# MLP weight groups with seven products: buffers of their own, other places, and 24 instead of 32 of them

## The chip, the cores and the metric

The kernel runs on one core of a Trainium2 chip. The metric is the device time of one execution in microseconds (us). The median of three runs of the kernel before is 1685.07 us (1681.4 to 1685.62). One more execution was recorded by the hardware profiler.

## What is computed

One decoder layer on 256 tokens of width 2048, all in float32. The change touches its last part only, the MLP:

```python
h2 = _rms(x, norm2_g)
x = x + jnp.square(jax.nn.relu(h2 @ w_up)) @ w_down
```

`w_up` is 2048 x 8192 and `w_down` 8192 x 2048. Before it, three token mixers (a gated convolution, forgetting attention, cross-attention to 256 memory tokens) are projected from x, gated, merged and multiplied by `w_out`.

## The kernel before

**Precision.** Each float32 operand is split in two parts of the type float32r: the upper part is a copy (ScalarE, `whi`), the lower part the difference between the value and the upper part (VectorE, `wlo`). A product takes three matmuls: lower x upper, upper x upper, upper x lower.

**Pieces and rings.** Weights stream from HBM in pieces of 256 rows x 512 columns (128 partitions x 2 x 512, 512 KB). There are four raw buffers, four of `whi` and four of `wlo` (RING = 4), all used by piece number modulo 4. SyncE issues the load of piece n when the lower part of piece n - 4 is made (L404 to L407, semaphore `lo_ready`). ScalarE makes the upper part of piece n (`split`, L527) when it has landed and TensorE has used piece n - 4 (`piece_used`); VectorE then makes the lower part (L882). Each engine works its queue strictly in the order in which it is written down.

**The MLP** is cut in 4 quarters of 4 blocks. Blocks 0 and 1 of a quarter multiply by `w_up` (1024 columns each), blocks 2 and 3 by `w_down`, with the quarter's activations as the left operand. A block has 8 groups (GROUPS) of 256 rows, each with a left and a right piece. A plain group (`half_group`, L1601) is 24 matmuls of 128x512. Groups 3 and 6 (`FAST`) are computed in another way (`fast_group`, L1621): a 2x2 by 2x2 block product with seven products instead of eight, 21 matmuls. It needs sums of weight blocks (`t_sums`, L1187 to L1192, VectorE, from the raw ring), their upper parts (`sums_hi`, L730, ScalarE) and lower parts (`sums_lo`, L1196, VectorE), the upper and lower parts of three of the four weight blocks (`split_fast`, L740 and L1203), and sums of the left operand (`s_sums`, `s_hi`, `s_lo`).

**Banks.** Of the eight PSUM banks, 0 to 3 hold the block's four results (C22, C12, C21, C11), 4 to 7 the products P5, P6, P7 and P1, which are summed over the block's two fast groups and combined with the rest at its end: ScalarE copies P1 (L835) and banks 0 to 3 (`c_copy`, L803), VectorE combines (`combine`, L1208 to L1212) and adds (`result`, L1230; for blocks 2 and 3 `x_to_sums`, L1224, first). Behind an up block, relu and square are taken (ScalarE, L813 and L816), and while the next block runs TensorE transposes the activations into banks 4 to 7 (`act_transposes`, L1406), from where ScalarE (`act_hi`, L707) and VectorE (`act_lo`, L920) take them. So the first fast group of a block must wait until the combination of the block before and these takings are done.

**Order.** VectorE's queue in a block (some lines left out), which fixes what stands behind a wait:

```python
                    left(blk, 2)
                    t_sums(ff_piece(q, blk, 3), 2 * at, base=by_8, base16=by16)
                    right(blk, 2)
                    sums_lo(2 * at, base=by_8)
                    if after_up:
                        act_lo(blk, 0)
                    fast(blk, 3)
                    if after_up:
                        act_lo(blk, 1)
                    left(blk, 4)
```

`left` and `right` make the lower part of a group's pieces, `fast` that of a fast group.

Of the kernel before, what the change touches and what calls it, by code (L numbers as in the profile page):

```python
# [18 lines left out]
F32 = mybir.dt.float32  # L19
# [137 lines left out]
FAST = (3, 6)  # L157
# [7 lines left out]
T_3, T_1, T_2, T_4 = range(4)  # L165


def ff_piece(q, blk=0, g=0):

    return first(B_FF) + FF_PIECES * q + 2 * (GROUPS * blk + g)  # L170
# [47 lines left out]
def build(nc, t, out):  # L218
    ctx = ExitStack()
    with ctx:  # L220
# [22 lines left out]
        with ExitStack() as mlp_only:  # L243
            comb = mlp_only.enter_context(nc.sbuf_tensor("comb", [P, 5, COLS], F32))
        y_parts, conv = two_views("y_parts", [P, 2, CW // P, TOK * P], F32R,
                                  "conv", [P, 2, CW // P, TOK * P], F32)
        with ExitStack() as mlp_only:
            def mlp(name, shape, dt):
                return mlp_only.enter_context(nc.sbuf_tensor(name, shape, dt))
            t_raw = mlp("t_raw", [P, 4, COLS], F32)  # L250
            t_hi = mlp("t_hi", [P, 4, COLS], F32R)
            t_lo = mlp("t_lo", [P, 4, COLS], F32R)
            s_up = mlp("s_up", [P, 2, len(FAST), 4, P], F32R)
            s_down = mlp("s_down", [P, 2, len(FAST), 4, P], F32R)
            s_raw = mlp("s_raw", [P, len(FAST), 4, P], F32)
            a_raw = mlp("a_raw", [P, len(FAST), 4, P], F32)
# [94 lines left out]
        t_used = sem("t_used")  # L351
# [13 lines left out]
        w_down = t["w_down"].rearrange("(q k p) n -> q p k n", p=P, k=KT)  # L365

# [32 lines left out]
        def _(sp):  # L399
# [66 lines left out]
            for n in range(ff_piece(0), ff_piece(1)):  # L466
                blk, g, side = (n - ff_piece(0)) // (2 * GROUPS), (n // 2) % GROUPS, n % 2
                k = slice(PK * g, PK * (g + 1))
                if blk < UPS:
                    load(n, w_up[:, k, WIDE * blk + COLS * side:WIDE * blk + COLS * (side + 1)])  # L470
                else:
                    at = WIDE * (blk - UPS) + COLS * side
                    load(n, w_down[0, :, k, at:at + COLS])

            with sp.Fori(0, QUARTERS - 1) as i:
                for n in range(ff_piece(1), ff_piece(2)):
                    blk, g, side = (n - ff_piece(1)) // (2 * GROUPS), (n // 2) % GROUPS, n % 2
                    k = slice(PK * g, PK * (g + 1))
                    if blk < UPS:
                        src = w_up[:, k, bass.ds(i * D + (D + WIDE * blk + COLS * side), COLS)]  # L480
                    else:
                        at = WIDE * (blk - UPS) + COLS * side
                        src = w_down[bass.ds(i + 1, 1), :, k, at:at + COLS].rearrange("q p k n -> (q p) k n")
                    load(n, src, base=i * FF_PIECES)
# [35 lines left out]
        def _(act):  # L520
            def split(n, base=0, base16=0):


                act.wait_ge(landed[n % RING], base16 + 16 * (n // RING + 1))
                if n >= RING:
                    act.wait_ge(piece_used, base + (n - RING + 1))
                act.activation(whi[n % RING], raw[n % RING], ACT.Copy).then_inc(hi_ready, 1)  # L527
# [183 lines left out]
            def a_copy(bk, u, gain=None):  # L711

                for j in range(PK):
                    last = act.activation(a_raw[:, u, 2 * j:2 * j + 2, :],
# [5 lines left out]
            def s_hi(i, u, dst, base=0):  # L720
                act.wait_ge(s_made, base * 4 + 4 * (i + 1))
                act.activation(dst[:, 0, u], s_raw[:, u], ACT.Copy).then_inc(s_hi_ready, 1)

            def sums_hi(i, base=0):

                if i is not None:
                    act.wait_ge(t_used, base + i)
                for h in range(2):
                    act.wait_ge(t_made, base * 3 + (3 * (i or 0) + 1 + 2 * h))
# [3 lines left out]
            def split_fast(n, base=0, base16=0):  # L733

                for u in range(2):
                    act.wait_ge(landed[(n + u) % RING], base16 + 16 * ((n + u) // RING + 1))
                act.wait_ge(piece_used, base + (n + 2 - RING))
                r = n % RING
                src, dst = [w[:, r:r + 2, :].rearrange("p r n -> p (r n)")[:, COLS:] for w in (raw_all, whi_all)]
                act.activation(dst, src, ACT.Copy).then_inc(hi_ready, 2)  # L740

            def wo_events(n):

                for j in range(NBD):
# [10 lines left out]
                    for a in range(2):  # L755
                        if n == e + 6 + a:
                            g, pair = G_X2 + 2 * j + a, 2 * j + a
                            if pair in FAST:
                                act.wait_ge(tr_made, g + 1)
                                a_copy(tr_bank(g), FAST.index(pair), R_N2 + PK * pair)  # L760
                            operand_hi(g, lhs_b, PK * pair, R_N2)
                if n == end(B_WO + FAST[0] // 2) + 10:
# [14 lines left out]
            def quarter(q, i):  # L777

                by_n, by16, by_b, by_8 = i * FF_PIECES, i * (FF_PIECES * 16 // RING), i * FF_BLOCKS, i * (2 * FF_BLOCKS)

                def left(blk, g):
                    split(ff_piece(q, blk, g), base=by_n, base16=by16)
                    if q == 0:
                        wo_events(ff_piece(q, blk, g))

                def right(blk, g):
                    split(ff_piece(q, blk, g) + 1, base=by_n, base16=by16)
                    if q == 0:
                        wo_events(ff_piece(q, blk, g) + 1)

                def fast(blk, g):
                    split_fast(ff_piece(q, blk, g), base=by_n, base16=by16)
                    if q == 0:
                        for side in range(2):
                            wo_events(ff_piece(q, blk, g) + side)

                def c_copy(blk, side):

                    at = FF_BLOCKS * q + blk
                    act.wait_ge(piece_used, by_n + (ff_piece(q, blk) - 1 + side))  # L800
                    act.wait_ge(ff_done, by_8 + 2 * (at - 1))
                    act.wait_ge(tr_made, by_8 + (G_FF + GROUPS * (q if blk else q - 1) + 4 * min((blk - 1) % FF_BLOCKS, UPS)))
# [15 lines left out]
                def act_hi(blk, side):  # L818
                    for a in range(2):
                        pair = 4 * (blk - 1) + 2 * side + a  # L820
                        g = G_FF + GROUPS * q + pair
                        if pair in FAST:
                            act.wait_ge(tr_made, by_8 + (g + 1))
                            a_copy(4 + 2 * side + a, FAST.index(pair))
                        plain_hi(g, PK * pair, act_parts, bk=4 + 2 * side + a, base=by_8)

                for blk in range(FF_BLOCKS):
                    after = q > 0 or blk > 0
                    after_up = 0 < blk <= UPS
                    at = FF_BLOCKS * q + blk  # L830
                    left(blk, 0)
                    if after:
                        act.wait_ge(piece_used, by_n + (ff_piece(q, blk) - 2))
                        act.wait_ge(ff_done, by_8 + 2 * (at - 1))
                        act.activation(comb[:, 3, :], bank[P1], ACT.Copy).then_inc(p1_copied, 1)  # L835
                    right(blk, 0)
                    if after:
                        c_copy(blk, 0)
                        c_copy(blk, 1)
                    left(blk, 1)  # L840
                    right(blk, 1)
                    if after_up:
                        relu_square(blk, 0)
                    left(blk, 2)
                    if after_up:
                        relu_square(blk, 1)
                    right(blk, 2)
                    sums_hi(2 * at, base=by_8)
                    if after_up:
                        act_hi(blk, 0)  # L850
# [867 lines left out]
```

## Time and profile before

| | us |
|---|---|
| median of 3 runs | 1685.07 |
| lowest, highest | 1681.4, 1685.62 |
| profiled execution | 1689.01 |
| its span, first to last instruction | 1687.3 |
| PE (matmuls) busy | 1642.3 |
| VectorE busy | 1104.8 |
| ScalarE busy | 851.2 |

The numbers behind an engine are the time in which it works, and PE's matmuls overlap: one lasts 390 ns and the next begins 227 ns after it. A wait is idle time ahead of an instruction, with what ended it. The granted clock is the share of TensorE's full clock (2.4 GHz) that the chip allowed; its other level is 1.2 GHz. "L882" is line 882 of the kernel before.

### The profile page before, as it was taken

How to read it: one execution, taken by the hardware profiler on the slowest of the kernel's cores; microseconds unless marked ns; L12 is line 12 of the kernel's file. 1: busy time of each engine (PE TensorE's matmuls, PEld its weight loads, DVE VectorE, ACT ScalarE, POOL GpSimd, SP SyncE). 2: the span in 40 equal slices, each digit the busy share in tenths (PEclk: the TensorE clock that was granted, in tenths of full speed). 3: DMA queues.
4: the chain of work that ended last, by engine and by line, in shares of the span. 5: the costliest groups of instructions: out<-in, count | busy, mean ns of one | idle time of the engine just before them, and what ended most of it. 6: DMA issues, size and time to landing. Idle time of an engine off the chain costs nothing.

```text
span 1687.3 us, 20278 instructions
## 1 busy us (share of the span) xinstructions
PE 1642.3 (97%) x7404; PEld 1354.5 (80%) x7404; DVE 1104.8 (65%) x1199; ACT 851.2 (50%) x1002; POOL 4.8 (0%) x13
## 2 busy tenths in 40 slices
PE   9999999999999999999999999999999999999997
PEld 7888888888888888888888877778777777877876
DVE  5856666555564444466656777777777786778777
ACT  6744444444454444444445566545554465446643
POOL 0000000000000000000000000000000000000000
PEclk9999999999999999999999999999999999999999
DMA  9856555565666666665566555466555555555554
GB/s 332 276 169 188 171 154 172 162 171 167 175 180 191 192 189 196 197 190 188 182 192 187 173 188 184 154 193 194 171 177 175 181 182 182 189 182 182 182 181 149
DMA packets 160190, 313.70 MB, mean 186 GB/s; under 512 B 9584, under 2 KB 9968, under 8 KB 159600
## 3 DMA queue, kind: packets, MB, share of 16 engines
q1 hardware_dynamic: 160112, 312.62, 60.2%
q8 instruction: 54, 0.88, 0.2%
q14 instruction: 24, 0.20, 0.0%
HBM read 310.49 MB, written 2.10 MB: 185 GB/s over the span
## 4 chain that ended last, share of the span: by engine, by line
PE 79%; DVE 8%; DMA 7%; issue 4%; ACT 1%; SPq 0%; DVEq 0%; ACTq 0%
PE bank L1389 51%; PE bank L1601 17%; PE bank L1621 8%; DMA raw<-in_w_down 4%; DVE wlo L882 3%; DMA raw<-in_w_up 2%; PE bank L1406 1%; DVE t_raw L1187 1%; ACT whi L527 1%; PE bank L1419 1%; DVE comb L1224 1%; DVE t_raw L1190 1%; DMA raw<-in_w_mem_kv 1%; DVE lhs_a L920 0%; DVE wlo L1203 0%
## 5 line engine op out<-in xcount | busy, mean ns | idle before, releaser
L882 DVE TENSOR_TENSOR wlo<-raw,whi 128x1024 fp32r<-128x1024 f32 x510 | 622.0, 1224 | 486.5 <-ACT whi L527 483.4
L527 ACT ACTIVATE whi<-raw 128x1024 fp32r<-128x1024 f32 x510 | 535.6, 1059 | 577.5 <-PE bank L1389 393.6
L1389 PE MATMUL bank<-whi,lhs_a 128*128 128x512 f32 x1920 | 598.2, 393 | 0.0
L1389 PEld LDWEIGHTS bank<-whi,lhs_a 128*128 128x128 f32 x1920 | 357.3, 188 | 71.7
L1389 PE MATMUL bank<-wlo,lhs_a 128*128 128x512 f32 x960 | 374.8, 390 | 0.0
L1601 PE MATMUL bank<-whi,lhs_a 128*128 128x512 f32 x768 | 238.5, 392 | 9.8 <-DVE wlo L882 9.8
L1601 PE MATMUL bank<-whi,lhs_b 128*128 128x512 f32 x768 | 238.5, 392 | 4.9 <-DVE wlo L882 4.9
L1389 PEld LDWEIGHTS bank<-wlo,lhs_a 128*128 128x128 f32 x960 | 180.3, 188 | 38.0
L1601 PEld LDWEIGHTS bank<-whi,lhs_a 128*128 128x128 f32 x768 | 143.1, 188 | 42.1 <-DVE wlo L882 13.2
L1601 PEld LDWEIGHTS bank<-whi,lhs_b 128*128 128x128 f32 x768 | 143.1, 188 | 36.3 <-DVE wlo L882 7.4
L1389 PE MATMUL bank<-whi,lhs_b 128*128 128x512 f32 x512 | 158.3, 391 | 2.7 <-DVE wlo L882 1.7
L1601 PE MATMUL bank<-wlo,lhs_b 128*128 128x512 f32 x384 | 149.8, 390 | 0.0
L1601 PE MATMUL bank<-wlo,lhs_a 128*128 128x512 f32 x384 | 149.8, 390 | 0.0
L730 ACT ACTIVATE t_hi<-t_raw 128x1024 fp32r<-128x1024 f32 x64 | 67.9, 1061 | 110.6 <-DVE t_raw L1187 98.9
L1389 PEld LDWEIGHTS bank<-whi,lhs_b 128*128 128x128 f32 x512 | 95.8, 188 | 23.1 <-issue 3.5
L1389 PE MATMUL bank<-wlo,lhs_b 128*128 128x512 f32 x256 | 99.8, 390 | 0.0
L1601 PEld LDWEIGHTS bank<-wlo,lhs_a 128*128 128x128 f32 x384 | 72.1, 188 | 15.1
L1601 PEld LDWEIGHTS bank<-wlo,lhs_b 128*128 128x128 f32 x384 | 72.1, 188 | 15.1
L1187 DVE TENSOR_TENSOR t_raw<-raw 128x1024 f32<-128x1024 f32 x32 | 39.1, 1223 | 62.3 <-DMA raw<-in_w_down 35.4
L1196 DVE TENSOR_TENSOR t_lo<-t_raw,t_hi 128x2048 fp32r<-128x2048 f32 x32 | 73.4, 2293 | 0.0
L1389 PEld LDWEIGHTS bank<-wlo,lhs_b 128*128 128x128 f32 x256 | 48.1, 188 | 10.0
L1203 DVE TENSOR_TENSOR wlo<-raw,whi 128x1536 fp32r<-128x1536 f32 x32 | 56.0, 1751 | 0.0
(201 smaller groups left out, 1285.4 us busy)
## 6 DMA issues: line engine op xcount, KB each, us to landing
raw<-in_w_in SPq DMA_DIRECT2D x208, 512.0 KB, 3.8
raw<-in_w_up SPq DMA_DIRECT2D x128, 512.0 KB, 4.0
raw<-in_w_down SPq DMA_DIRECT2D x128, 512.0 KB, 4.4
raw<-in_w_out SPq DMA_DIRECT2D x32, 512.0 KB, 4.1
raw<-in_w_mem_kv SPq DMA_DIRECT2D x30, 512.0 KB, 6.6
raw<-in_w_conv_out SPq DMA_DIRECT2D x16, 512.0 KB, 4.8
raw<-in_w_fox_out SPq DMA_DIRECT2D x16, 512.0 KB, 4.5
raw<-in_w_mem_out SPq DMA_DIRECT2D x16, 512.0 KB, 4.3
```

The lines of the kernel that those rows point to most:

```text
L527: act.activation(whi[n % RING], raw[n % RING], ACT.Copy).then_inc(hi_ready, 1)
L730: act.activation(t_hi[:, 2 * h:2 * h + 2, :], t_raw[:, 2 * h:2 * h + 2, :], ACT.Copy).then_inc(t_hi_ready, 1)
L882: dve.tensor_tensor(wlo[n % RING], raw[n % RING], whi[n % RING].bitcast(F32), ALU.subtract).then_inc(lo_ready, 1)
L1187: dve.tensor_tensor(t_raw[:, 0:2, :], b[:, 1:3, :], b[:, 0:1, :].to_broadcast([P, 2, COLS]), ALU.subtract).then_inc(t_made, 1)
L1190: dve.tensor_tensor(t_raw[:, T_2, :], t_raw[:, T_1, :], b22, ALU.add).then_inc(t_made, 1)
L1196: dve.tensor_tensor(t_lo[:], t_raw[:], t_hi[:].bitcast(F32), ALU.subtract).then_inc(t_lo_ready, 1)
L1203: dve.tensor_tensor(lo, src, hi.bitcast(F32), ALU.subtract).then_inc(lo_ready, 2)
L1224: last = dve.tensor_tensor(v, v, x_half(c, side), ALU.add)
L1389: last = pe.matmul(dst, lhs[:, part, k + kk, s], w[:, kk, :], start=(k + kk == 0 and i == 0), stop=(k + kk == tiles - 1 and i == 2))
L1406: last = pe.transpose(bank[tr_bank(g) if bk is None else bk][:, P * i:P * (i + 1)], src, ident[:])
L1601: last = pe.matmul(bank[2 * side + tok], lhs[:, part, PK * g + kk, P * tok:P * (tok + 1)], w[:, kk, :], start=(g + kk == 0 and i == 0), st ...
L1621: ins = pe.matmul(bank[at], a[part], b[w_part], start=(own and u == 0 and i == 0), stop=(own and u == len(FAST) - 1 and i == 2))
```

## The change

- Places of a block are told apart from the rows that they use: K_ORDER gives the row group of each place. Fast groups stand at places 4 and 7 in blocks 0 and 2 and at place 4 alone in blocks 1 and 3 (FAST_AT), 24 instead of 32 in all. Their row groups are 3 and 7.
- The raw weights of a fast group go to `raw_f`, one buffer of 1 MB (both pieces). The raw ring of four holds plain pieces alone (`plain(n) % RING`). `whi` and `wlo` stay as they are. The pair of the next fast group is loaded when the lower part of the fast group before is made. SyncE's order of loads is sorted by what frees each buffer.
- `fast_group` computes C21, C12 and C11 first, and waits for banks 4 to 7 behind them; then P1, P6, P7, P5. It reports each product (`fast_made`), so that copies and combination can begin sooner. The combination is cut in three parts.
- The queues of ScalarE and VectorE are written out block by block in a new order. The transposes of block 1 stand before the left and right pieces of place 2, those of block 2 before the right piece of place 1 and the left of place 2.
- `a_raw` and `s_raw` hold one group instead of two. The source of `w_down` in the loop is addressed by rows; the bytes are the same.

```diff
-FAST = (3, 6)
+
+K_ORDER = (0, 1, 2, 4, 3, 5, 6, 7)
+FAST_AT = ((4, 7), (4,), (4, 7), (4,))
+FAST_K = (3, 7)
+FASTS = sum(len(at) for at in FAST_AT)
...
+def freed_by(n):
+
+    if is_fast(n):
+        return max(m for m in range(first(B_FF), n - n % 2) if is_fast(m))
+    return max(m for m in range(n) if not is_fast(m) and plain(m) == plain(n) - RING)
+
+
+def load_order(q):
+
+    head = [ff_piece(q), ff_piece(q) + 1]
+    head += [ff_piece(q, 0, FAST_AT[0][0]) + side for side in range(2)]
+    return head + sorted((n for n in range(ff_piece(q), ff_piece(q + 1)) if n not in head),
+                         key=lambda n: (freed_by(n), n))
...
+                if is_fast(n):
+                    if n == ff_piece(0, 0, FAST_AT[0][0]):
+                        sp.wait_ge(merged_ready, NBD)
+                    elif n > ff_piece(0, 0, FAST_AT[0][0]) + 1:
+                        sp.wait_ge(lo_ready, base + (freed_by(n) + 1))
+                    side = n % 2
+                    sp.dma_start(raw_f[:, PK * side:PK * (side + 1), :], src).then_inc(fast_landed, 16)
+                    return
+                sp.wait_ge(lo_ready, base + (freed_by(n) + 1))
+                slot = plain(n) % RING
+                sp.dma_start(raw[slot], src).then_inc(landed[slot], 16)
...
+            def t_upper(f, n_before, base=0, base_n=0):
+
+                if n_before is not None:
+                    act.wait_ge(piece_used, base_n + (n_before + 1))
...
+            def fast_upper(n, f, base=0, base_f=0):
+
+                act.wait_ge(fast_landed, base_f * 32 + 32 * (f + 1))
                 act.wait_ge(piece_used, base + (n + 2 - RING))
...
+                lower(1, 0)
+                t_of(1, 4)
+                sums(0, 0, 1)
+                left(1, 1)
+                sums(0, 2)
+                right(1, 1)
+                up_result(0, 0)
+                up_result(0, 1)
+                lower(1, 2)
+                t_lo_of(1, 4)
+                act_lo(1, 0)
+                lower(1, 3)
+                act_lo(1, 1)
+                fast(1, 4)
...
+                t_of(2, 7)
+                lower(2, 6)
+                t_lo_of(2, 7)
+                fast(2, 7)
+
+
+                lower(3, 0)
+                t_of(3, 4)
+                sums(2, 0, 1)
+                left(3, 1)
+                sums(2, 2)
+                right(3, 1)
+                x_to_sums(FF_BLOCKS * q + 2, 0, base=by_b)
+                lower(3, 2)
+                t_lo_of(3, 4)
+                down_result(q, 2, 0)
+                down_result(q, 2, 1)
+                lower(3, 3)
+                fast(3, 4)
...
-                product(P5, s1, t1)
-                product(P6, s2, t2)
-                product(P7, s3, t3)
-                product(C21, a22, t4).then_inc(t_used, 1)
+                pe.wait_ge(t_lo_ready, fast_index(q, blk, at) + 1)
+                product(C21, a22, t4)
                 pe.wait_ge(lo_ready, n + 2)
-                product(C12, s4, b22)
-                product(P1, a11, b11)
-                product(C11, a12, b21).then_inc(piece_used, 2)
+                product(C12, s4, b22).then_inc(fast_made, 1)
+                product(C11, a12, b21).then_inc(fast_made, 1)
+                if begins:
+
+                    number = FF_BLOCKS * q + blk
+                    if number == 0:
+                        pe.wait_ge(dve_emptied, emptied(B_FF - 1))
+                        pe.wait_ge(tr_taken, G_FF)
+                    else:
+                        pe.wait_ge(combined, 3 * number)
+                        if 0 < blk <= UPS:
+                            pe.wait_ge(tr_taken, G_FF + GROUPS * q + 4 * blk)
+                product(P1, a11, b11).then_inc(fast_made, 1)
+                product(P6, s2, t2).then_inc(fast_made, 1)
+                product(P7, s3, t3).then_inc(fast_made, 1)
+                product(P5, s1, t1).then_inc(piece_used, 2)
```

## Rows read from the trace of the kernel before

**Rows 1.** The page: span, busy time by engine, GB/s in 40 slices.

```profile
span 1687.3 us, 20278 instructions
...
PE 1642.3 (97%) x7404; PEld 1354.5 (80%) x7404; DVE 1104.8 (65%) x1199; ACT 851.2 (50%) x1002; POOL 4.8 (0%) x13
...
GB/s 332 276 169 188 171 154 172 162 171 167 175 180 191 192 189 196 197 190 188 182 192 187 173 188 184 154 193 194 171 177 175 181 182 182 189 182 182 182 181 149
```

**Rows 2.** PE's waits: line, released by, us in total, times, longest.

```profile
PE bank L1601 <- DVE wlo L882: 14.7, 14, 1.7
PE bank L1621 <- DVE lhs_a L920: 11.1, 4, 3.1
PE bank L1621 <- issue: 8.4, 4, 3.3
```

**Rows 3.** PE's timeline, start and length: MLP's first and last matmul, one transpose batch.

```profile
938.16 0.62 PE L1601 MATMUL bank<-whi,lhs_b 128*128 128x512 f32 x2
...
989.45 1.03 PE L1406 MATMUL bank<-ident,stage 128*128 128x128 f32 x8
990.24 0.71 PE L1601 MATMUL bank<-whi,lhs_b 128*128 128x512 f32 x2
...
1680.31 0.39 PE L1601 MATMUL bank<-wlo,lhs_a 128*128 128x512 f32 x1
```

**Rows 4.** Windows: length, busy of PE, PEld, DVE, ACT, POOL, granted clock, DMA.

```profile
960.20:971.08 10.88, 10.88 (x49) 9.02 (x48) 9.46 (x9) 6.57 (x6) 0.00 (x0) 1.00 0.48 142
1048.18:1055.82 7.64, 7.64 (x21) 6.05 (x22) 2.91 (x6) 0.63 (x1) 0.00 (x0) 0.61 0.81 273
...
1649.86:1652.71 2.85, 2.85 (x12) 2.37 (x13) 2.85 (x2) 2.23 (x2) 0.00 (x0) 1.00 0.51 150
```

**Rows 5.** PE's timeline: a fast group behind a wait, second quarter, block 1.

```profile
1188.31 1.19 PE L1621 MATMUL bank<-t_hi,s_up 128*128 128x512 f32 x2 [3.31 <-issue]
```

**Rows 6.** VectorE's timeline before the first wait of rows 5.

```profile
1178.04 1.22 DVE L1187 TENSOR_TENSOR t_raw<-raw 128x1024 f32<-128x1024 f32 x1 [3.73 <-DMA raw<-in_w_up]
...
1180.64 1.22 DVE L882 TENSOR_TENSOR wlo<-raw,whi 128x1024 fp32r<-128x1024 f32 x1
1181.85 2.29 DVE L1196 TENSOR_TENSOR t_lo<-t_raw,t_hi 128x2048 fp32r<-128x2048 f32 x1
1184.06 1.28 DVE L920 TENSOR_TENSOR lhs_a<-bank,lhs_a 128x512 fp32r<-128x512 f32 x2
1185.26 1.75 DVE L1203 TENSOR_TENSOR wlo<-raw,whi 128x1536 fp32r<-128x1536 f32 x1
...
1188.12 1.22 DVE L882 TENSOR_TENSOR wlo<-raw,whi 128x1024 fp32r<-128x1024 f32 x1
```

**Rows 7.** VectorE's timeline around a block's start: combine, pieces, x_to_sums.

```profile
1308.18 0.69 DVE L1208 TENSOR_TENSOR comb<-bank,comb 128x512 f32<-128x512 f32 x1
...
1309.62 1.22 DVE L1212 TENSOR_TENSOR comb<-comb,bank 128x1024 f32<-128x1024 f32 x1
1310.76 1.22 DVE L882 TENSOR_TENSOR wlo<-raw,whi 128x1024 fp32r<-128x1024 f32 x1
...
1314.33 2.35 DVE L1224 TENSOR_TENSOR comb<-comb,x_sb 128x1024 f32<-128x1024 f32 x2
```

**Rows 8.** DMA: page's issues (KB each, median us), landing in 1160 to 1215.

```profile
raw<-in_w_up SPq DMA_DIRECT2D x128, 512.0 KB, 4.0
raw<-in_w_down SPq DMA_DIRECT2D x128, 512.0 KB, 4.4
...
DMA to landing us min/median/max: 3.6/4.2/7.2
```

**Rows 9.** ScalarE's timeline: upper parts of two pieces, relu, a fast group's upper part.

```profile
1167.80 2.00 ACT L527 ACTIVATE whi<-raw 128x1024 fp32r<-128x1024 f32 x2
1169.69 1.32 ACT L813 ACTIVATE stage<-stage,sm 128x512 f32<-128x512 f32 x2
...
1202.58 1.47 ACT L740 ACTIVATE whi<-raw 128x1536 fp32r<-128x1536 f32 x1
```

More of the change, by code:

```diff
@@ L465, in _, with load_ff @@
                 load_block(b)
[L466 to L473, printed above, removed]
+            def load_ff(n, src, base=0):
+                if is_fast(n):
[9 more added lines that the diff above has]
+                sp.dma_start(raw[slot], src).then_inc(landed[slot], 16)
@@ new lines, in quarter @@
+                upper(0, 0)
+                if q:
+                    c_copy(0, 0)
+                left(0, 1)
+                if q:
+                    c_copy(0, 1)
+                right(0, 1)
+                t_hi_of(0, 4)
+                upper(0, 2)
+                upper(0, 3)
+                fast(0, 4)
+                upper(0, 5)
+                if q == 0:
+                    s_hi(1, 1, s_up)
+                left(0, 6)
+                t_hi_of(0, 7)
+                right(0, 6)
@@ new lines, in quarter @@
+                fast(0, 7)
+                upper(1, 0)
+                c_copy(1, 0)
+                c_copy(1, 1)
+                p1_copy((q, 0, FF_BLOCKS * q))
+                upper(1, 1)
+                t_hi_of(1, 4)
+                upper(1, 2)
+                relu_square(1, 0)
+                relu_square(1, 1)
+                left(1, 3)
+                act_hi(1, 0)
+                right(1, 3)
+                act_hi(1, 1)
+                fast(1, 4)
+                upper(1, 5)
+                s_hi(2 * q + 2, 0, s_down, base=2 * i)
@@ new lines, in quarter @@
+                act_hi(2, 1)
+                fast(2, 4)
+                upper(2, 5)
+                s_hi(2 * q + 3, 1, s_down, base=2 * i)
+                left(2, 6)
+                t_hi_of(2, 7)
+                right(2, 6)
+                fast(2, 7)
+                upper(3, 0)
+                c_copy(3, 0)
+                c_copy(3, 1)
+                p1_copy((q, 2, FF_BLOCKS * q + 2))
+                upper(3, 1)
+                t_hi_of(3, 4)
+                upper(3, 2)
+                upper(3, 3)
@@ new lines, in quarter @@
+                lower(0, 1)
+                if q:
+                    down_result(q - 1, 3, 0)
+                    down_result(q - 1, 3, 1)
+                lower(0, 2)
+                t_lo_of(0, 4)
+                lower(0, 3)
+                fast(0, 4)
+                lower(0, 5)
+                if q == 0:
+                    s_sums(1)
+                t_of(0, 7)
+                left(0, 6)
+                if q == 0:
+                    s_lo(1, 1, s_up)
+                right(0, 6)
@@ new lines, in quarter @@
+                lower(1, 5)
+                s_lo(2 * q + 2, 0, s_down, base=2 * i)
+                t_of(2, 4)
+                lower(1, 6)
+                sums(1, 0, 1, 2)
+                left(1, 7)
+                t_lo_of(2, 4)
+                right(1, 7)
+                lower(2, 0)
+                up_result(1, 0)
+                left(2, 1)
+                up_result(1, 1)
+                right(2, 1)
+                lower(2, 2)
+                act_lo(2, 0)
+                lower(2, 3)
@@ L1358, in _ @@
+                lower(3, 2)
[3 more added lines that the diff above has]
+                lower(3, 3)
+                fast(3, 4)
+                lower(3, 5)
+                lower(3, 6)
+                sums(3, 0, 1, 2)
+                x_to_sums(FF_BLOCKS * q + 3, 1, base=by_b)
+                lower(3, 7)
             quarter(0, 0)
```

468 lines of the change are left out of this document (231 added, 237 removed).

## The prediction

> **What bounds the kernel now.** I read the page first, then the waits of TensorE, then TensorE's timeline, then the queues of VectorE and ScalarE around its waits. The page [rows 1] says that PE is busy for 1642.3 of 1687.3 us, so only two things move the time: how many matmuls there are, and where PE waits. The waits of PE [rows 2] are nearly all in the MLP: 14.7 us before plain groups (L1601) and 11.1 + 8.4 us before groups with seven products (L1621), 34.2 us in 22 places. The MLP runs from its first matmul at 938.16 to the end of its last at 1680.31 + 0.39 = 1680.70 [rows 3], 742.5 us.
>
> How much of it is needed? In a stretch without waits, 48 matmuls take 10.88 us [rows 4], so the pitch is 0.2267 us. There are 16 blocks with six plain groups of 24 matmuls and two fast ones of 21: 16 x 186 = 2976 matmuls, 674.6 us. Sixteen batches of eight transposes take 0.79 us each (989.45 to 990.24), and the twelve matmuls behind one run about 0.10 us long [rows 3]: 14.2 us; two smaller batches of the last x2 transposes add 0.9 us. Sum 689.7 us. The other 52.8 us are lost: 34.1 us of waits, and 18.7 us in which PE works at less than its pitch. The second part follows the first: after the wait that ended at 1048.18 a fast group took 7.64 us at a granted clock of 0.61, that is partly at 1.2 GHz, where 21 x 0.2267 = 4.76 us are needed [rows 4]. So a wait of about 3 us [rows 2] can cost 2.9 us again.
>
> Where the waits come from shows in VectorE's queue before the wait of 3.31 us that ended at 1188.31 [rows 5]. VectorE stood 3.73 us for the DMA of the next fast group's weights (1178.04), then worked without a pause: sums, a plain piece, t_lo, four operand passes, the fast group's lower part, until 1188.1 [rows 6]. PE started right behind it. The t sums read the raw ring, whose four pieces are freed only when lower parts are made, so a fast group's two pieces are always loaded late. The same pattern (t_raw behind a DMA) is what precedes the other waits that I followed.
>
> **The change, part by part.**
> 1. Fast groups: 32 become 24. Eight groups get 3 matmuls more: 24 x 0.2267 = +5.4 us, with nothing that hides it, as it is PE's own time. This is certain.
> 2. VectorE and ScalarE do less. A fast group costs VectorE 1180.64 - 1178.04 = 2.60 (sums) + 2.21 (t_lo) + 1.67 (lower part) = 6.5 us, two plain pieces 2 x 1.14 = 2.3 us [rows 6, 7]: 8 x 4.2 = 34 us less on an engine that is 65% busy. Worth nothing by itself; it gives slack.
> 3. raw_f, a raw buffer for fast groups alone, so that the plain ring keeps four plain pieces. The pair for the next fast group is issued when the lower part of the one before is made. A 512 KB load lands after 4.0 to 4.4 us in the median, at most 7.2 us in one stretch [rows 8]; the fastest slice moved 332 GB/s [rows 1], so the second of two loads comes 0.52 MB / 332 = 1.6 us behind. I take 4.4 + 1.6 = 6.0 us for the pair (bounds 4.4, as if it were one, and 7.2). SyncE's order of issue is sorted by what frees each piece, so I find no load queued behind one that must wait longer. Bytes stay the same.
> 4. New order. c-copies and the combination of P1, P5 to P7 move, and the fast group starts with the three products that go to the C banks, so that banks 4 to 7 are needed 2.0 us later. The transposes move one to two pieces back, same cost. PE's six increments of a semaphore per fast group add no wait of their own.
>
> Now I lay the queues against a PE that never waits, block by block, with rows' lengths: plain group 5.44 us, fast 4.76, DVE plain piece 1.14, combine 0.72 + 0.72 + 1.14, x_to_sums 2.28, a result 1.14 [rows 7]; ACT piece 1.0, fast upper 1.5, relu (two passes) and square 2.3 [rows 9]; zero is a block's start on PE.
>
> Block 0: everything is 2 us early or more. Its second fast group has t_of bound by the pair issued at the lower part of the group at place 4; t_lo is ready 2 us before PE wants it.
>
> Block 1: the pair is issued at about -7.1, lands at -1.5 (up weights, 4.0 + 1.6). DVE: t_of until 1.1, combine parts until 2.5, left(1,1) at 3.7 (PE wants it at 5.4), then combine, right, first result at 7.8. ACT's relu and square end at 10.1, and PE wants the transposes' input at 10.9. Slack 0.8 us. The fast group at place 4 is ready 2 us early, and the banks' wait, which set the price in [rows 5], is over at 18.3 for a need at 23.4.
>
> Block 2: the first fast group's pair had the whole of block 1, nothing waits. The lower part of the one at place 7: ScalarE may make its upper part from 33.6 (end of group 5 frees the slots) to 35.0, VectorE makes t_lo until 35.5 and the lower part until 37.2; PE wants it at 39.0. The block lasts 43.8, so the pair for block 3 is issued at -6.5.
>
> Block 3: the pair lands at -6.5 + 6.0 = -0.5. Behind it VectorE has without a pause t_of 2.6, combine 1.44, left(1) 1.14, combine 1.14, right(1) 1.14, x_to_sums 2.28, two pieces 2.28, t_lo 2.21, two results 2.28, left(3) 1.14: 17.65, so the left piece of group 3 is made at 17.2. PE wants it at 16.3. That is the place that is late next: 0.9 us, at most 7.2 - 6.0 more; with 4.4 us for the pair it is gone. With hand-overs between engines I take 1.1 us, four times 4.4 us. It is short, and the waits before plain groups, at most 1.7 us [rows 2], show no drop of the clock behind them: 12 matmuls behind one of them took 2.85 us at a granted clock of 1.00, where 2.72 are needed [rows 4].
>
> Sum. 3000 x 0.2267 = 680.0, transposes 15.1: 695.1 us, from 938.16 to 1633.3. After the last matmul come 1687.3 - 1680.7 = 6.6 us of results and stores, unchanged since place 7 of the last block is plain both times: 1639.9, and 1.7 us of what lies around the span (1689.0 against 1687.3): 1641.6. With 4.4 us in block 3: 1646.0 against a profiled 1689.0, so -43. The median of the runs before is 1685.1, 3.9 us under the profiled one; most of the lost clock goes, so I expect less of that spread and take 1 us off: 1645.0.
>
> The Trainium skill, page "DMA: Bandwidth & Descriptors", section "Anatomy of one DMA", puts a transfer at about 2.0 us plus bytes over 436 GB/s. By it a pair would be an estimated 4.4 us, block 3 would not wait, and the sum would be 1641. Its measured table (section "Bandwidth") has 6.15 us of transfer for 1 MB, by which block 3 would wait about 1 us as above. The trace's 4.2 us median for 512 KB is above the 3.2 us of the formula; I go by the trace.
>
> **The rivals.** A (forecast): the old waits go, block 3 stays about 1 us short. 1638 to 1652. B: the pair's landing and VectorE's chain behind it decide more than once a quarter. With 7.2 us instead of 6.0, block 3 loses 2.3, block 1 0.8 (the transposes' input) and the two groups at place 7 a little, some 3.5 to 5 us a quarter with one slow-clock stretch of 1 to 2.9 us now and then: 1641.6 + 14 to 25 = 1655 to 1667. For it: VectorE is the engine with the longest chain, and loads issued in a burst showed 7.2 us. Against it: on most places I find 2 us of slack and a lighter queue. C: the plain ring is the true cause and raw_f does not cure it, half of the loss stays: 1641.6 + 26 = 1668 to 1680. Against it: in the walk each plain piece is issued 4 us or more before ScalarE wants it. D, the slower side: raw_f has one buffer, and each refill becomes a wait of PE. By the walk PE begins to wait when a pair takes over 5.1 us (block 3), 6.4 (block 1) and 7.8 (place 7 of blocks 0 and 2), sum 27.1. It decides at about 8 us of landing: four refills per quarter then cost 4 x 8 - 27.1 = 4.9 us, and two drops of the clock 5.8 us, together 10.7, which times four is the whole gain. At 9 us it is 1641.6 + 4 x 14.7 = 1700. The longest landing that a row shows is 7.2 us, and that in a burst of four which the new order spreads. E: gain and loss cancel, near 1685.
>
> **How the numbers follow.** A 0.62, B 0.23, C 0.07, D 0.05, E 0.03. The time is A's, 1645.0. The range takes all of A and more than half of B: low 1637 (A without any wait and with the 4 us by which the median may lie under the profile), high 1663. Changes under 0.3%, 5 us, can't be told from none. Faster A + B + C = 0.92, same 0.03, slower 0.05.
>
> **What would show it.** PE's matmul count in the MLP up by 24; no "t_hi, s" group with a wait of over 1.5 us ahead of it, so the two L1621 rows of [rows 2] gone; mean granted clock 0.99 to 1.0 in the MLP; VectorE's t_raw still waits for a DMA, but PE does not follow; PE waits left before group 3 of block 3, some 4 times about 1 us, on wlo. Blocks 43 to 45 us long. The forecast is wrong if PE waits before fast groups, or before the transposes in block 1 (relu and square late), or if pairs take over 7 us to land.

## The result and the profile after

The changed kernel takes 1643.89 us (median of 4 runs, 1643.75 to 1646.03) against 1685.34 us (4 runs, 1681.4 to 1686.15): ratio 0.9762, 95% interval 0.9744 to 0.9779. Forecast were 1645.0 us and a range of 1637 to 1663. The profiled execution took 1646.03 us, its span is 1644.3 us. The forecast for the changed kernel held, in part because two errors in its sum cancel. The experiments show that the reason is narrower than the change: the new buffer, put into the old order of the queues with 32 fast groups, gives 49 us, and what the change adds to that takes about 8 of them back. In the first experiment one of the ten runs took 1818.23 us at a granted clock of 0.852; it is left out of the ratio.

The page and PE's waits after the change, which answer to [rows 1] and [rows 2]; the L1785 of these rows is a plain group, the fast one is L1806:

```profile
span 1644.3 us, 20222 instructions
...
PE 1630.8 (99%) x7428; PEld 1349.2 (82%) x7428; DVE 1071.4 (65%) x1175; ACT 840.9 (51%) x994; POOL 4.8 (0%) x13
...
PE bank L1785 <- DVE wlo L1006: 3.8, 5, 1.0
```

Matmuls rose from 7404 to 7428, the 24 forecast. The waits in the MLP fell from 34.2 us in 22 places to 3.8 us in 5, and none stands before a fast group. The five on PE's timeline, with the first and last matmul of the MLP and, from the windows, the MLP as a whole (its columns are those of [rows 4]):

```profile
938.54 0.62 PE L1785 MATMUL bank<-whi,lhs_b 128*128 128x512 f32 x2
...
1087.23 0.73 PE L1785 MATMUL bank<-whi,lhs_a 128*128 128x512 f32 x2 [0.48 <-DVE wlo L1006]
...
1261.44 0.73 PE L1785 MATMUL bank<-whi,lhs_a 128*128 128x512 f32 x2 [0.26 <-DVE wlo L1006]
...
1436.39 0.74 PE L1785 MATMUL bank<-whi,lhs_a 128*128 128x512 f32 x2 [1.00 <-DVE wlo L1006]
...
1600.72 0.73 PE L1785 MATMUL bank<-whi,lhs_a 128*128 128x512 f32 x2 [1.02 <-DVE wlo L1006]
...
1613.14 0.73 PE L1785 MATMUL bank<-whi,lhs_a 128*128 128x512 f32 x2 [1.01 <-DVE wlo L1006]
...
1639.57 0.39 PE L1785 MATMUL bank<-wlo,lhs_a 128*128 128x512 f32 x1
```

```profile
938.54:1639.96 701.42, 697.61 (x3137) 576.33 (x3135) 525.62 (x508) 395.83 (x440) 0.00 (x0) 1.00 0.59 188
```

All five lie in block 3 of a quarter, and the granted clock is 1.00 through the MLP. Four of them, one in each quarter, stand before group 3, where the prediction put them. The fifth (1600.72) stands in the fourth quarter before the left piece of group 1. There VectorE had waited 3.68 us for the pair:

```profile
1595.54 1.23 DVE L1308 TENSOR_TENSOR t_raw<-raw_f 128x1024 f32<-128x1024 f32 x1 [3.68 <-DMA raw_f<-in_w_down]
```

That is 7.7 us after the issue of this pair at 1587.86, where the prediction had taken 6.0. This is rival B in one place. The longest landing of a single `raw_f` load in this run was 8.1 us (median 4.8), in another place, where PE did not wait; "pairs take over 7 us to land" was one of the prediction's signs of being wrong.

The chain that the prediction laid out for block 3 stands in VectorE's queue. The first quarter's (here the start of the piece that PE waited for is 1085.96, and PE's wait ended at 1087.23):

```profile
1069.56 1.23 DVE L1308 TENSOR_TENSOR t_raw<-raw_f 128x1024 f32<-128x1024 f32 x1 [1.18 <-DMA raw_f<-in_w_down]
...
1076.95 2.35 DVE L1351 TENSOR_TENSOR comb<-comb,x_sb 128x1024 f32<-128x1024 f32 x2
...
1081.49 2.28 DVE L1317 TENSOR_TENSOR t_lo<-t_raw,t_hi 128x2048 fp32r<-128x2048 f32 x1
1083.69 1.22 DVE L1357 TENSOR_TENSOR x_sb<-stage,comb 128x1024 f32<-128x1024 f32 x1
1084.83 1.22 DVE L1357 TENSOR_TENSOR x_sb<-junk,comb 128x1024 f32<-128x1024 f32 x1
1085.96 2.35 DVE L1006 TENSOR_TENSOR wlo<-raw,whi 128x1024 fp32r<-128x1024 f32 x2
```

From 1069.56 to the end of the left piece at 1087.2 VectorE has no pause: 17.6 us, where the prediction added up 17.65.

### The profile page after: what moved, and what is told of

Same layout as the page of the kernel before. It is cut to its first block, busy times and chain, and to the rows that moved or that the text cites. A ratio compares the mean times of both kernels' runs of the same rounds, so it can differ in the third digit from the quotient of the medians.

```text
span 1644.3 us, 20222 instructions
## 1 busy us (share of the span) xinstructions
PE 1630.8 (99%) x7428; PEld 1349.2 (82%) x7428; DVE 1071.4 (65%) x1175; ACT 840.9 (51%) x994; POOL 4.8 (0%) x13
## 4 chain that ended last, share of the span: by engine, by line
PE 90%; DVE 4%; DMA 2%; issue 2%; ACT 1%; SPq 0%; DVEq 0%; ACTq 0%
PE bank L1572 52%; PE bank L1785 28%; PE bank L1806 6%; PE bank L1589 2%; DMA raw_f<-in_w_down 1%; DVE wlo L1006 1%; DVE t_lo L1317 1%; PE bank L1602 1%; DMA raw<-in_w_mem_kv 1%; DVE x_sb L1357 1%; DVE comb L1351 0%; ACT whi L589 0%; DVE wlo L1323 0%; ACT t_hi L792 0%; DVE t_raw L1308 0%
## 5 line engine op out<-in xcount | busy, mean ns | idle before, releaser
L1006 DVE TENSOR_TENSOR wlo<-raw,whi 128x1024 fp32r<-128x1024 f32 x526 | 638.7, 1223 | 463.1 <-ACT whi L589 460.0
L589 ACT ACTIVATE whi<-raw 128x1024 fp32r<-128x1024 f32 x526 | 554.4, 1058 | 597.6 <-PE bank L1572 394.8
L1572 PE MATMUL bank<-whi,lhs_a 128*128 128x512 f32 x1920 | 597.8, 392 | 0.0
L1785 PE MATMUL bank<-whi,lhs_a 128*128 128x512 f32 x832 | 257.7, 391 | 3.8 <-DVE wlo L1006 3.8
L1785 PE MATMUL bank<-whi,lhs_b 128*128 128x512 f32 x832 | 257.1, 390 | 0.0
L1785 PEld LDWEIGHTS bank<-whi,lhs_a 128*128 128x128 f32 x832 | 155.1, 188 | 37.9 <-DVE wlo L1006 6.3
L1785 PEld LDWEIGHTS bank<-whi,lhs_b 128*128 128x128 f32 x832 | 155.4, 188 | 31.8
L1572 PE MATMUL bank<-whi,lhs_b 128*128 128x512 f32 x512 | 158.3, 390 | 3.8 <-DVE wlo L1029 2.1
L1785 PE MATMUL bank<-wlo,lhs_b 128*128 128x512 f32 x416 | 162.0, 389 | 0.0
L1785 PE MATMUL bank<-wlo,lhs_a 128*128 128x512 f32 x416 | 162.0, 389 | 0.0
L1572 PEld LDWEIGHTS bank<-whi,lhs_b 128*128 128x128 f32 x512 | 95.6, 188 | 24.6 <-issue 5.1
L1572 PE MATMUL bank<-wlo,lhs_b 128*128 128x512 f32 x256 | 99.7, 389 | 0.0
L1785 PEld LDWEIGHTS bank<-wlo,lhs_b 128*128 128x128 f32 x416 | 78.1, 188 | 16.4
L1785 PEld LDWEIGHTS bank<-wlo,lhs_a 128*128 128x128 f32 x416 | 78.1, 188 | 16.3
L800 ACT ACTIVATE whi<-raw_f 128x1536 fp32r<-128x1536 f32 x24 | 35.7, 1489 | 65.8 <-PE bank L1785 65.8
L1323 DVE TENSOR_TENSOR wlo<-raw_f,whi 128x1536 fp32r<-128x1536 f32 x24 | 42.1, 1755 | 38.9 <-ACT whi L800 38.7
L1317 DVE TENSOR_TENSOR t_lo<-t_raw,t_hi 128x2048 fp32r<-128x2048 f32 x24 | 54.8, 2284 | 0.0
L598 ACT ACTIVATE wide<-bank,sm 128x512 f32<-128x512 f32 (+1 forms) x48 | 30.4, 686 | 36.8 <-PE bank L1572 36.4
```

What stands on the lines that cost most here:

```text
L589: act.activation(whi[n % RING], raw[slot], ACT.Copy).then_inc(hi_ready, 1)
L598: last = act.activation(outs[tok], src, func, scale=scale[:, tok:tok + 1])
L800: act.activation(whi_all[:, r:r + 2, :].rearrange("p r n -> p (r n)")[:, COLS:], raw_f[:, 1:4, :].rearrange("p k n -> p (k n)"), ACT.Copy) ...
L1006: dve.tensor_tensor(wlo[n % RING], raw[plain(n) % RING], whi[n % RING].bitcast(F32), ALU.subtract).then_inc(lo_ready, 1)
L1317: dve.tensor_tensor(t_lo[:], t_raw[:], t_hi[:].bitcast(F32), ALU.subtract).then_inc(t_lo_ready, 1)
L1323: dve.tensor_tensor(lo, raw_f[:, 1:4, :].rearrange("p k n -> p (k n)"), hi.bitcast(F32), ALU.subtract).then_inc(lo_ready, 2)
```

## The experiments

**The count alone.** In the kernel before, blocks 1 and 3 lose the fast group at place 6:

```diff
+FAST_IN = ((3, 6), (3,), (3, 6), (3,))
-                        if g in FAST:
+                        if g in FAST_IN[blk]:
```

> The kernel before with one part of the change alone: blocks 1 and 3 of a quarter have one fast group (place 3), not two; 24 in all, raw ring, order and places as before. Theory (the late landing of the fast groups' weights in the shared ring makes the waits): PE's own work rises by 24 x 0.2267 = 5.4 us; the waits before the fast groups at place 3 of blocks 1 and 2 stay (19.5 us in 8, with most of the 18.7 us of slow clock), the one before group 6 of block 3 goes (4 x 1.2) and that of block 0's start may shrink; 1680 to 1690 us, no gain. Rival (the count alone relieves VectorE, and that is where the gain comes from): most of the 41 us is here, 1650 us or less.

1682.87 us against 1686.17, ratio 0.998 (0.9962 to 0.9998). PE's waits:

```profile
PE bank L1640 <- DVE lhs_a L933: 10.7, 4, 3.5
PE bank L1620 <- DVE wlo L895: 9.1, 10, 1.5
PE bank L1640 <- issue: 7.7, 4, 2.8
```

The eight waits before fast groups stay (18.4 us against 19.5). A VectorE with less work does not cure them, and the count is not where the gain is.

**The buffer in the old order.** The changed kernel with 32 fast groups at places 3 and 6 and the old order of the queues, written as the old loop over blocks. From the change it keeps four things: `raw_f`, the sorted loads, the new order of the seven products with the bank wait behind the third, and the report of each product. So it is not the buffer by itself.

```diff
-K_ORDER = (0, 1, 2, 4, 3, 5, 6, 7)
-FAST_AT = ((4, 7), (4,), (4, 7), (4,))
-FAST_K = (3, 7)
+K_ORDER = tuple(range(8))
+FAST_AT = ((3, 6),) * 4
+FAST_K = (3, 6)
-            turns = {(1, 2, 0): 0, (1, 2, 1): 1, (2, 1, 1): 0, (2, 2, 0): 1}
+            turns = {(1, 1, 1): 0, (1, 2, 0): 1, (2, 1, 1): 0, (2, 2, 0): 1}
```

> The buffer alone: raw_f, the sorted loads and the product-by-product reports of the changed kernel, with 32 fast groups at places 3 and 6 and the queues' order of the kernel before (row groups in natural order). The bank wait stands behind the first three products as in the changed kernel. Theory (late weights made the waits): VectorE's waits for the t sums fall from 62 us to under 25 and PE's waits from 34 to under 12, no more slow clock, 1640 to 1655 us; the last combination no longer ends behind PE, so the tail is about 4.3 us and not 6.6. Rival (the order of the queues and the places did it): 1665 us or more.

1636.08 us against 1684.94, ratio 0.9706 (0.968 to 0.9733): better than I expected, and faster than the changed kernel, whose interval in the first comparison begins at 0.9744. PE waits nowhere in the MLP, and VectorE never waits for a DMA before the t sums. The MLP in the windows, the landings of raw_f, and one of its t sums in VectorE's queue:

```profile
940.78:1630.96 690.18, 690.18 (x3113) 572.43 (x3111) 559.46 (x534) 407.12 (x448) 0.00 (x0) 1.00 0.60 191
```

```profile
DMA to landing us min/median/max: 3.7/4.6/6.4
```

```profile
1180.36 1.23 DVE L963 TENSOR_TENSOR wlo<-raw,whi 128x1024 fp32r<-128x1024 f32 x1 [3.07 <-ACT whi L589]
1181.50 0.68 DVE L1258 TENSOR_TENSOR s_down<-s_raw,s_down 128x512 fp32r<-128x512 f32 x1
1182.10 1.22 DVE L1265 TENSOR_TENSOR t_raw<-raw_f 128x1024 f32<-128x1024 f32 x1
```

690.2 us is, within 0.5, the 689.7 us that the prediction gave as PE's own work for 32 groups. So 742.5 us went down to nothing but work, with VectorE as busy as before (559 us) and in the same order.

Could the new order of the products be the cause here and not the buffer? The old order asks for the banks before the first product. They are free when VectorE has taken the last transposes; in block 1 of the second quarter that is at 1172.81 + 1.28 = 1174.09, and PE begins the fast group at 1174.30, without a wait:

```profile
1172.81 1.28 DVE L1001 TENSOR_TENSOR lhs_a<-bank,lhs_a 128x512 fp32r<-128x512 f32 x2
```

```profile
1174.30 0.62 PE L1728 MATMUL bank<-t_hi,lhs_b 128*128 128x512 f32 x2
```

In all eight such places the banks were free about 0.2 us before PE began. By these rows a bank wait ahead of the group would cost next to nothing, but the margin is thin, and no run put it there in the old order.

Against the changed kernel, profile against profile, the span is 8.5 us shorter (1635.8 against 1644.3). The MLP is 11.2 us shorter (690.18 against 701.42); it begins 2.2 us later, and the tail is 0.5 us longer.

**Back to 32 groups in the new order.**

```diff
-FAST_AT = ((4, 7), (4,), (4, 7), (4,))
+FAST_AT = ((4, 7),) * 4
```

with the start of block 1 (t sums, combination in parts, results) used for all blocks.

> The changed kernel with the part on the count undone: all four blocks of a quarter have fast groups at places 4 and 7 (32), from raw_f, with the changed kernel's order for a block that follows a block with a fast group at its end, now in all blocks; the transposes of block 2 stand where those of block 1 do. Theory: PE needs 5.4 us less than in the changed kernel, 1636 us without waits, but now every block begins with the chain pair landing, t sums, combination, pieces, which was 0.3 to 1.0 us late in block 3 and had 0.8 us of slack in block 1; blocks 3 and 0 of a quarter lose 1 to 2 us each, block 2 about 1, and waits of 2 us may bring the slow clock: 1640 to 1660. Rival (count decides): near or above 1670.

1660.46 us, ratio 0.9849 (0.9824 to 0.9874), just above the 1640 to 1660 that I expected: 12.7 us of waits in blocks 3 and 0, three of 2.4 us with a dropped clock behind them, and 10.2 us behind the last matmul, because the last group is now a fast one.

```profile
PE bank L1800 <- DVE wlo L1009: 12.7, 9, 2.4
...
1487.45 1.22 PE L1800 MATMUL bank<-whi,lhs_b 128*128 128x512 f32 x2 [2.42 <-DVE wlo L1009]
```

Then the same with VectorE's work that nobody waits for moved back:

```diff
                 fast(0, 4)
+                if q:
+                    x_to_sums(FF_BLOCKS * q - 1, 1, base=by_b)
+                    down_result(q - 1, 3, 0)
+                    down_result(q - 1, 3, 1)
...
                 fast(3, 4)
+                down_result(q, 2, 0)
+                down_result(q, 2, 1)
```

> The kernel with 32 fast groups from raw_f at places 4 and 7, with the x sums and results of the down blocks moved behind the fast group's lower part in blocks 0 and 3. In the run without this move PE waited 12.7 us, all in those blocks, lost 8 us of clock behind three waits of 2.4 us, and had a tail of 10.2 us because the last group is a fast one. Theory: the waits and the slow clock go, PE's own work is 5.4 us less than in the changed kernel, the tail stays 5.9 us longer: 1639 to 1645 us. Rival (VectorE has no room for 32 such groups): waits move to other places, 1650 or more.

1643.86 us, ratio 0.9757 (0.9731 to 0.9783), in the range. One wait of 0.6 us is left, the tail is 10.3 us (1630.8 to 1641.1). VectorE has room for 32 groups; what made PE wait was the order of its work.

**The late refill.** SyncE waits for two more lower parts before it issues a pair:

```diff
-                        sp.wait_ge(lo_ready, base + (freed_by(n) + 1))
+                        sp.wait_ge(lo_ready, base + (freed_by(n) + 3))
```

> The changed kernel, but SyncE issues each pair for raw_f two lower parts later (it waits for lo_ready two counts higher), some 3 to 4 us at a block's start. It measures the price of a late refill. By my walk: block 3 loses the 3.9 us in full on top of its 0.3 to 1.0, block 1 about 3, the places 7 of blocks 0 and 2 about 0.8 each, 8 to 9 us a quarter, and two slow-clock stretches of 1 to 2.9 us: 36 to 55 us more, 1680 to 1700 us, that is all the gain gone. Rival (the refill has slack that I did not see, the gain is from the order of the queues): under 1655.

1716.62 us, ratio 1.0181 (1.0144 to 1.0218): 73 us above the changed kernel, more than the 36 to 55 expected, and slower than the kernel before. PE's waits, two rows of VectorE's wait for raw_f, and the MLP in the windows:

```profile
PE bank L1785 <- DVE wlo L1006: 52.4, 20, 5.6
```

```profile
DVE t_raw L1308 <- DMA raw_f<-in_w_down: 68.1, 12, 6.8
...
DVE t_raw L1308 <- DMA raw_f<-in_w_up: 45.7, 8, 8.1
```

```profile
940.14:1713.97 773.83, 721.34 (x3137) 589.03 (x3135) 524.10 (x508) 398.63 (x440) 0.00 (x0) 0.97 0.54 170
```

Waits 52.4 us, and 773.8 - 52.4 = 721.4 us of matmul work, where the changed kernel took 697.6 us: 24 us more. The windows put about 22 us down to the dropped clock. I worked this out from windows of 3 us through the MLP: each loses its length times what its granted clock lacks to 1.00.

I had expected 8 to 9 us of waits a quarter and 8 to 23 us of slow clock in all. The clock stayed within that; the waits are 13.1 us a quarter. The pairs for the two places 7 make 4.1 of them and not 1.6, and there are five waits a quarter, not four, the fifth worth 2.0 us on average: the pair for block 2, to which I had given the whole of block 1, is read by t_of(2, 4), which stands ahead of group 6's pieces in VectorE's queue. In the first quarter it started at 1022.12 behind a wait of 5.13 us:

```profile
1022.12 1.23 DVE L1308 TENSOR_TENSOR t_raw<-raw_f 128x1024 f32<-128x1024 f32 x1 [5.13 <-DMA raw_f<-in_w_down]
```

**The bank wait first.**

```diff
+                if begins:
...
+                        pe.wait_ge(combined, 3 * number)
                 pe.wait_ge(t_lo_ready, fast_index(q, blk, at) + 1)
                 product(C21, a22, t4)
```

> The changed kernel, but the first fast group of a block waits for banks 4 to 7 (combination of the block before, transposes taken) before its first product and not before its fourth. Theory: the banks are free 5 us before they are wanted, so nothing changes: 1644, within 1 us. Rival (starting with the C banks is what removed the waits of L1621): PE waits before the fast groups at place 4 of blocks 1 and 2 again, 1650 or more.

1644.24 us, ratio 0.9761 (0.9741 to 0.9782), waits of 2.9 us in 4 places, all in block 3. In the changed kernel the new order of the products is worth nothing for PE's waits. I read the "DVE lhs_a" and "issue" waits of [rows 2] as VectorE's lateness seen from PE, which came from its own wait for the DMA [rows 6].

**Block 3's results later.** On one chip, with the changed kernel itself:

```diff
                 lower(3, 3)
                 fast(3, 4)
+                down_result(q, 2, 0)
+                down_result(q, 2, 1)
```

> The changed kernel unchanged, as the reference of this set on the same chip: 1643 to 1646 us.

> The changed kernel, but in block 3 VectorE makes the two results of block 2 after the fast group's lower part and not before group 3's pieces, 2.28 us out of the chain that was late. Theory: PE's five waits before group 3 of block 3 (3.8 us in the profiled run, 0.3 to 1.0 each) go, and nothing else becomes late since ScalarE copies need those results only in the next block: 2 to 4 us less than the unchanged one. Rival (the waits come from the raw pieces' landing and not from VectorE's chain): no change.

The changed kernel 1643.51 us (1641.94 to 1645.49), this one 1639.9 (1639.21 to 1640.03), both 5 runs: 3.6 us less, and PE has no wait in the MLP. A second set, on another chip, gave it 1641.54 us (1639.63 to 1642.94), there with one wait of 0.8 us in its profile. That one stands in the fourth quarter before group 1 of block 3, behind a VectorE that had waited 3.42 us for the pair: it is the fifth wait again, which lies ahead of the moved results in VectorE's queue. So the four waits before group 3 were VectorE's chain in block 3, as the prediction had it, and the fifth is the pair's landing.

> The same as the run with the results later, on the chip of this set, as the measure for the two-part version: 1639 to 1641 us.

**One load of 1 MB.**

```diff
-                    side = n % 2
-                    sp.dma_start(raw_f[:, PK * side:PK * (side + 1), :], src).then_inc(fast_landed, 16)
+                    sp.dma_start(raw_f[:].rearrange("p (k s) n -> p k (s n)", k=PK),
+                                 src).then_inc(fast_landed, 16)
```

> The changed kernel with raw_f filled by one load of 1 MB instead of two of 512 KB (its four weight blocks stand in another order, the work is the same). By the Trainium skill, page DMA: Bandwidth & Descriptors, a larger transfer shares one fixed cost. From rows: two loads take one issue of 0.37 us more than one, so I expect the pair to land at most 0.4 us earlier, VectorE's waits for raw_f (25 us in 19) to fall by a third, and the time by 0 to 1.5 us. Rival (one load of 1 MB is spread worse over the queues): later landing, PE waits in block 3 over 1.5 us, 1 to 5 us more.

> The changed kernel with both changes that gained: results of block 2 later and one load of 1 MB per fast group. PE had no wait left in the MLP with the first one alone, so the second should add nothing: within 1 us of it, 1639 to 1641 us. If the one load gave its 2 us by another way than PE's waits, it would be 1638 or less.

Alone 1641.8 us (1641.3 to 1645.86), together with the later results 1640.07 (1639.75 to 1640.46). The issues of raw_f (KB each, median us to landing), first in the changed kernel, then with one load, and VectorE's waits for it in the same order:

```profile
raw_f<-in_w_up SPq DMA_DIRECT2D x24, 512.0 KB, 4.9
raw_f<-in_w_down SPq DMA_DIRECT2D x24, 512.0 KB, 4.7
...
DVE t_raw L1308 <- DMA raw_f<-in_w_down: 14.7, 12, 3.7
...
DVE t_raw L1308 <- DMA raw_f<-in_w_up: 10.3, 7, 2.3
```

```profile
raw_f<-in_w_up SPq DMA_DIRECT2D x12, 1024.0 KB, 5.1
raw_f<-in_w_down SPq DMA_DIRECT2D x12, 1024.0 KB, 5.1
...
DVE t_raw L1314 <- DMA raw_f<-in_w_down: 9.2, 11, 1.6
...
DVE t_raw L1314 <- DMA raw_f<-in_w_up: 7.5, 7, 1.7
```

VectorE's waits fall from 25.0 to 16.7 us, a third, as expected, and PE's from some 3 to 0.7. By itself it gains about 1.7 us, which the spread of the runs (1641.94 to 1645.49 for the changed kernel) does not clear; once block 3 has slack it adds nothing that these runs can tell.

**The combination later.**

```diff
-                sums(3, 0, 1, 2)
-                x_to_sums(FF_BLOCKS * q + 3, 1, base=by_b)
                 lower(3, 7)
+                sums(3, 0, 1, 2)
+                x_to_sums(FF_BLOCKS * q + 3, 1, base=by_b)
```

> The changed kernel, but the combination of block 3 (P1 copy, three sums, x added) is moved from before to after the last group's pieces. It tests why the tail behind the last matmul fell from 6.6 to 4.3 us: in the kernel before, the last fast group was at place 6 and the combination ended 0.3 us after PE. Theory: the tail grows by 1 to 2.5 us, in the rest of the quarters the combination has slack until the fast group of the next block and costs 0 to 1 us: 1645 to 1647 us. Rival (the tail fell for another reason, such as the stores): no change in the tail.

1642.38 us (1642.1 to 1644.09), no change, and a miss: the tail is still 4.3 us, since the last pieces are made at 1629.4 and the combination (1629.35 to 1634.41) is over before PE is (1637.96):

```profile
1628.09 0.58 ACT L878 ACTIVATE comb<-bank 128x512 f32<-128x512 f32 x1
...
1632.05 2.36 DVE L1351 TENSOR_TENSOR comb<-comb,x_sb 128x1024 f32<-128x1024 f32 x2
```

## Why the prediction was right, point by point

**The count.** 5.4 us: 24 matmuls more, as said, and kernels without waits in the MLP show their price. With 24 groups the MLP takes 696.25 us with the later results and 695.62 us with the one load as well, against 690.18 us with 32 groups: 5.4 to 6.1 us. The second of them in the windows:

```profile
938.01:1633.63 695.62, 695.62 (x3137) 577.11 (x3135) 525.74 (x508) 396.23 (x440) 0.00 (x0) 1.00 0.59 189
```

**The waits and the clock.** 34.1 and 18.7 us were to go and 4.4 to come in block 3: 3.8 came, the clock is 1.00. This was the larger part of the gain, and its mechanism, the late landing, held: with the buffer in the old order all of it is gone. The prediction read the whole 18.7 us as slow clock. Windows of 3 us through the MLP of the kernel before give about 14 us of slow clock, behind six of the eight waits before fast groups. The other 5 us are what a wait costs beyond its row. The row begins when the last matmul ends, 0.39 us after its start, while the next could have begun after 0.23; and the first pair behind a wait takes about 0.73 us and not 0.62. That is some 0.27 us for each of the 22 waits.

**Block 3.** For four of the five waits place, cause and size were right (0.3 to 1.0 us each against 1.1), shown by moving 2.3 us out of the chain. The fifth came from a pair that took 7.7 us; the sum had no term for it.

**The part that was mis-sized: the tail.** I carried 6.6 us over as unchanged. It is 4.3 us (1639.96 to 1644.3). In the kernel before, ScalarE's copy of P1 waited for the count of the whole group, and the result of the left side began only when the combination had ended, behind PE's end at 1680.70:

```profile
1675.29 0.60 ACT L872 ACTIVATE comb<-bank 128x512 f32<-128x512 f32 x1 [1.90 <-PE bank L1621]
...
1678.63 2.36 DVE L1224 TENSOR_TENSOR comb<-comb,x_sb 128x1024 f32<-128x1024 f32 x2
1681.03 1.23 DVE L1366 TENSOR_TENSOR x_sb<-bank,comb 128x1024 f32<-128x1024 f32 x1
```

With the buffer in the old order, the last fast group is again at place 6, but P1 is copied when its product is made, 1623.51, and the combination ends at 1629.47, before PE's 1630.96; the tail is 4.8 us. So P1's earlier place among the products and the report by product together are worth about 1.8 us at the end (6.6 against 4.8); I did not part the two. Of this, 1.4 us show in VectorE's queue: the result of the right side began 1.47 us behind PE's end in the kernel before (1682.17) and 0.03 us behind it here. The rest lies behind that result, and its cause stays open. Where block 3's combination stands in the queue is not what matters. Against these 2.3 us stands what I left out in the MLP: it began at 938.54 and not 938.16, and its work was 697.6 us, not 695.1. The kernels without waits need 695.6 to 696.3 us for the same matmuls, so 1.3 to 2.0 us of this belong to the waits, some 0.3 to 0.4 us for each of the five. The two errors cancelled: that the sum came out at the profiled 1646.0 to the tenth is luck.

**The median.** I took 1 us off the profiled time; the other three runs lie 2.1 to 2.3 us under it.

**What I did not see.** I weighed the change as a whole and never set its buffer against the old order. My part 2 said that less work for VectorE "gives slack", my part 4 let the new order pass without a price. Neither the lower count nor the new order of the queues was needed: the old order has no wait with 32 groups. I put it down to where the t sums stand. A pair is issued when the lower part of the fast group before is made. In the old order three plain pieces lie between that and the next t sums in the same block, seven across blocks. Between the two stand 7.9 us or more everywhere in the MLP, and the slowest load of that run landed after 6.4 us. In the new order it is two pieces for five of the six pairs of a quarter, and VectorE waits 25.0 us in 19 places for data of which PE makes use only one to six groups later. This reading fits the rows; a run of the new order with the t sums alone moved later was not made, nor the new order with the shared ring.

**The rivals.** C (raw_f does not cure the ring) is refuted by the result and by the buffer in the old order. B, a pair that lands late, came true in one place of the fourth quarter and cost about 1 us there. D's mechanism is real: with a refill two lower parts later the kernel is 1.8% slower than before. Its price was about right. With 6.0 us for the pair and the 3.9 us that I took for the delay, its sum is 4 x 9.9 - 27.1 = 12.5 us of waits and 5.8 us of clock a quarter, 1715 us in all; 13.1 and about 5.5 were measured, 1716.6 us. The sum came out in spite of two faults in its parts: it has no fifth place (block 2), and the waits at places 7 are larger than it has them. What was too low was my expectation for that run, 8 to 9 us of waits a quarter. No run stands near the break-even that I set at 8 us. That the range held with D at 0.05 rests on landings that stayed at a median of 4.8 us.

## What to carry to other kernels

When PE waits for VectorE, read VectorE's queue upwards to its own last wait: here the waits of PE in the MLP of the kernel before began with a DMA into a ring slot that was freed late. Give the odd consumer its own raw buffer first and time that, before work is taken away or queues are rewritten: a change that gains 41 us held a smaller one that gains 49. Put an instruction that waits for a load as late in its queue as its own reader allows, and move what nobody waits for behind it.

## What the runs showed of the hardware that I had not expected

Short waits cost no clock, longer ones often do, but not each time. Behind waits of up to 1.0 us the granted clock stayed 1.00 in the changed kernel, and in the kernel before it also did so behind waits of 1.47 and 1.76 us. Behind three waits of 2.4 us with 32 groups in the new order the pitch rose to that of 1.2 GHz (two matmuls in up to 1.22 us instead of 0.62). In the late refill a wait of 3.49 us had no drop behind it and one of 4.21 us had; the two windows, beginning where the waits ended:

```profile
1266.53:1273.50 6.97, 6.97 (x31) 5.76 (x32) 6.19 (x5) 4.26 (x4) 0.00 (x0) 1.00 0.48 150
...
1286.65:1294.00 7.35, 7.35 (x21) 5.84 (x22) 7.35 (x7) 1.54 (x2) 0.00 (x0) 0.62 0.51 150
```

Taken together, PE's waits are worth about 1.5 times their length, both in the kernel before (34.1 us brought 18.7 more) and in the late refill (52.4 brought 24).

A load of 1 MB landed after 5.1 us in the median, where one of two loads of 512 KB in a pair landed after 4.7 to 4.9. The Trainium skill, page "DMA: Bandwidth & Descriptors", section "Anatomy of one DMA — SWDGE (gpsimd) path", gives 2.0 us plus bytes over 436 GB/s for one transfer issued by GpSimd, an estimated 4.4 us for 1 MB. The trace, with loads issued by SyncE and others in flight, has 0.7 us more.
